# A two-layer hybrid attention step on one core: bias table in contiguous runs; scaling, shifting and evacuation moved to ScalarE, low parts to VectorE

## The reference

```python
def rms_norm(x, g):
    y = xf * lax.rsqrt(jnp.mean(xf * xf, axis=-1, keepdims=True) + EPS)
    return y * g
def modulate(x, g, shift, scale):
    return rms_norm(x, g) * (1 + scale[:, None, :]) + shift[:, None, :]
def gated_residual(x, y, g, gate):
    return x + gate[:, None, :] * rms_norm(y, g)
def channel_mixer(h, w1, w2):
    return jnp.square(jax.nn.relu(h @ w1)) @ w2
...
# per layer, for the context tokens (c_ctx) and the latent tokens (c):
h = modulate(x, g[0], shift0, scale0)
y = mixer(h)      # layer 0: retention heads || neighbourhood attention; layer 1: latent attention
x = gated_residual(x, y, g[1], gate)
h = modulate(x, g[2], shift1, scale1)
x = gated_residual(x, channel_mixer(h, w_mlp_in, w_mlp_out), g[3], gate1)
# neighbourhood attention adds to each score a value of a table of 15 x 31 per head:
bias = rpb[:, dr, dc]; bias = jnp.where(valid, bias, NEG_INF)
```

## Time and profile before

| | us |
|---|---|
| three runs | 2003.93, 2004.2, 2000.57 (median 2003.93) |
| the profiled execution | 2003.88 |
| its span | 2002.1 |
| TensorE busy | 1825.5 (91%) |
| VectorE busy | 1160.4 (58%) |
| ScalarE busy | 698.1 (35%) |
| GpSimd busy | 272.1 (14%) |

### The profile page before, as it was taken

How to read it: one execution, slowest core, us unless ns; L and a number is a source line. 1 busy time by engine, 2 the same in 40 slices (tenths; PEclk the granted TensorE clock), 3 DMA queues, 4 the chain that set the end, 5 groups by cost and what they waited for, 6 DMA issues and landing times.

```text
span 2002.1 us, 28780 instructions
## 1 busy us (share of the span) xinstructions
PE 1825.5 (91%) x11572; PEld 1647.5 (82%) x11572; DVE 1160.4 (58%) x2017; ACT 698.1 (35%) x1179; POOL 272.1 (14%) x262
## 2 busy tenths in 40 slices
PE   7899988379879999999988899999898999999998
PEld 3799853259779999999977886777787999999997
DVE  2777557364776676767574765565457653233345
ACT  2332234154442222313333454555444313132233
POOL 2200000142420000000242120011242000000012
PEclk9799989589889999999988799999998899999999
DMA  8244320102334545444331020000132442222232
GB/s 293 88 158 148 105 62 12 43 1 87 93 98 134 159 136 155 140 153 142 106 88 56 27 85 1 1 1 1 56 103 74 131 122 74 75 73 82 72 111 74
DMA packets 274605, 181.32 MB, mean 91 GB/s; under 512 B 23029, under 2 KB 249130, under 8 KB 274474
## 3 DMA queue, kind: packets, MB, share of 16 engines
q1 hardware_dynamic: 274474, 179.50, 29.3%
HBM read 175.92 MB, written 3.56 MB: 90 GB/s over the span
## 4 chain that ended last, share of the span: by engine, by line
PE 70%; DVE 11%; issue 5%; SPq 5%; ACT 5%; POOL 3%; DMA 1%; ACTq 0%; POOLq 0%; DVEq 0%
PE ps L630 18%; PE ps L632 18%; PE ps L631 18%; SPq L552 4%; PE ps L1099 4%; PE ps L1077 3%; DVE nt L1570 2%; ACT w_hi L414 2%; PE ps L1088 2%; PE ps L701 1%; DVE w_lo L423 1%; DVE nt L1568 1%; POOL rstd L2101 1%; DVE xT L1558 1%; PE ps L762 1%
## 5 line engine op out<-in xcount | busy, mean ns | idle before, releaser
L630 PE MATMUL ps<-hM_hi,w_lo 128*128 128x320 f32 x1120 | 361.9, 323 | 36.2 <-POOL hM_lo L2105 20.7
L414 ACT ACTIVATE w_hi<-stage 128x1024 fp32r<-128x1024 f32 (+2 forms) x230 | 239.2, 1040 | 405.3 <-PE ps L632 355.8
L423 DVE TENSOR_TENSOR w_lo<-stage,w_hi 128x1024 fp32r<-128x1024 f32 (+2 forms) x230 | 281.5, 1224 | 164.8 <-ACT w_hi L414 162.9
L630 PE MATMUL ps<-h_hi,w_lo 128*128 128x320 f32 x1152 | 359.8, 312 | 4.7 <-DVE w_lo L423 4.6
L632 PE MATMUL ps<-h_hi,w_hi 128*128 128x320 f32 x1152 | 357.2, 310 | 0.0
L631 PE MATMUL ps<-h_lo,w_hi 128*128 128x320 f32 x1152 | 357.1, 310 | 0.0
L631 PE MATMUL ps<-hM_lo,w_hi 128*128 128x320 f32 x1120 | 355.0, 317 | 0.0
L632 PE MATMUL ps<-hM_hi,w_hi 128*128 128x320 f32 x1120 | 354.6, 317 | 0.0
L630 PEld LDWEIGHTS ps<-hM_hi,w_lo 128*128 128x128 f32 x1120 | 216.7, 194 | 49.5 <-POOL hM_lo L2105 27.7
L2101 POOL TENSOR_TENSOR rstd<-rstd,sq 128x320 f32<-128x320 f32 x98 | 118.3, 1207 | 990.6 <-ACT sq L1148 987.5
L630 PEld LDWEIGHTS ps<-h_hi,w_lo 128*128 128x128 f32 x1152 | 217.0, 188 | 9.5 <-DVE w_lo L423 7.4
(11 more groups left out here) (287 smaller groups left out, 2928.3 us busy)
## 6 DMA issues: line engine op xcount, KB each, us to landing
stage<-in_w_mlp_in SPq DMA_DIRECT2D x76, 512.0 KB, 4.0
stage<-in_w_mlp_out SPq DMA_DIRECT2D x76, 512.0 KB, 4.2
slab_mlp<-in_w_ada SPq DMA_DIRECT2D x28, 1024.0 KB, 5.1
stage<-in_w_in_ac SPq DMA_DIRECT2D x28, 512.0 KB, 3.7
slab_ac<-in_w_ada SPq DMA_DIRECT2D x12, 1024.0 KB, 5.9
ada_a<-in_w_ada SPq DMA_DIRECT2D x8, 1024.0 KB, 8.6
stage<-in_w_out_ac SPq DMA_DIRECT2D x14, 512.0 KB, 4.1
stage<-in_w_out_c SPq DMA_DIRECT2D x14, 512.0 KB, 4.0
```

Source lines behind the costliest of these rows:

```text
L414: nc.scalar.activation(w_hi[:, n % 2, 0:width], stage[:, n % STAGE, 0:width], ACT.Copy)\
L423: nc.vector.tensor_tensor(w_lo[:, n % 2, 0:width], stage[:, n % STAGE, 0:width], w_hi[:, n % 2, 0:width].bitcast(F32), ALU.subtract).then_ ...
L630: mm(out, lo[:, k], xh, start=j == 0, stop=False)
```

## The change

1. The bias table has rows of 8 x 31 words without gaps, 272 words per head. Each of the 128 DMAs puts 8 runs of 248 words instead of 64 runs of 31. GpSimd reads the window with a hand-built view that steps 31 words from key row to key row.
2. A modulated tile: VectorE makes the product with the spread factor; ScalarE scales and shifts it twice, into the high part and, in place, into `nt`; VectorE subtracts for the low part. GpSimd has no part in it.
3. `project_out`: ScalarE squares PSUM directly and then copies it into `yT`; VectorE has no part in it.
4. At units 0, 5, 6 and 7 of the first up stage of each layer, GpSimd and not VectorE makes the plain square `s2`.

```diff
-STAGES = (..., ("out0", 8, "sweeps", "d"),
+STAGES = (..., ("out0", 8, "sweeps", "a"),      # who evacuates; out1 likewise
+BIAS_W = ROWS * RPB_C + 24
+POOL_SQUARES = (0, 5, 6, 7)
-        [bias] = lay(80, ("bias", [P, NH, ROWS, 48], F32))
+        [bias] = lay(80, ("bias", [P, NH, BIAS_W], F32))
-                    sp.dma_start(bias[q:q + 1, :, :, c + 1:c + 1 + RPB_C],
-                                 rpb[0:1, :, ROWS - 1 - r:2 * ROWS - 1 - r, :]).then_inc(na_bias_in, 16)
+                    sp.dma_start(bias[q:q + 1, :, c + 1:c + 1 + ROWS * RPB_C],
+                                 rpb[0:1, :, ROWS - 1 - r:2 * ROWS - 1 - r, :].rearrange("l h r c -> l h (r c)"))
+                        .then_inc(na_bias_in, 16)
 # ScalarE
-                f(out[:, k, half(s)], nt[:, k % 2, half(s)], ACT.Copy).then_inc(h_hi_done[s], 1)
+                for dst, done in ((out, None), (nt, h_hi_done[s])):
+                    for a, b, g in HALVES[s]:
+                        to = dst[:, k, a:b] if done is None else dst[:, k % 2, a:b]
+                        last = f(to, nt[:, k % 2, a:b], ACT.Identity, scale=coef[:, layer, which, k, g:g + 1],
+                                 bias=mod[:, layer, 8 * shift + k, g:g + 1])
+                last.then_inc(h_hi_done[s], 1)
 # ScalarE, project_out, every unit u
-                    if u:
-                        y_square(y_name, name, u - 1)
+                    act.wait_ge(unit_done, g + 1)
+                    square(y_name, s, u % 8, single(g))
+                    f(yT[:, j, half(s)], single(g), ACT.Copy).then_inc(act_evac, 1)
 # VectorE
-                link(tt(nt[:, k % 2, cols], xT[:, k, cols], spread(name, s), ALU.mult))
-                for a, b, g in HALVES[s]:
-                    last = ts(nt[:, k % 2, a:b], nt[:, k % 2, a:b], coef[...], mod[...], ALU.mult, ALU.add)
-                last.then_inc(h_full[s], 1)
+                tt(nt[:, k % 2, cols], xT[:, k, cols], spread(name, s), ALU.mult).then_inc(h_full[s], 1)
+            def low_part(name, s, k, hi, lo):
+                dve.wait_ge(h_hi_done[s], KD * MOD_NO[name] + k + 1)
+                tt(lo[:, k, cols], nt[:, k % 2, cols], hi[:, k, cols].bitcast(F32), ALU.subtract)
+                    .then_inc(h_lo_done[s], 1)
+            def modulate(name, s, k, hi, lo):
+                normalise(name, s, k)
+                if k:
+                    low_part(name, s, k - 1, hi, lo)
+                if k == KD - 1:
+                    low_part(name, s, k, hi, lo)
 # GpSimd
-                        bias[:, 2 * m + e, :, u:u + KW].rearrange("p r c -> p c r"),
+                        bias_window(2 * m + e, u),
+                at = bias[:, h, u:u + 1]
+                return bass.AP(at.tensor, at.offset, [at.ap[0], [1, KW], [RPB_C, ROWS]])
```

More of the change, by code:

```diff
@@ L1156, in square_root, with operand @@
                     .then_inc(root_done[s], 1)
-            def operand(name, s, k, out):
+            def operand(name, layer, which, shift, s, k, out):
                 act.wait_ge(h_full[s], KD * MOD_NO[name] + k + 1)
-                f(out[:, k, half(s)], nt[:, k % 2, half(s)], ACT.Copy).then_inc(h_hi_done[s], 1)
+                for dst, done in ((out, None), (nt, h_hi_done[s])):
[4 more added lines that the diff above has]
+                last.then_inc(h_hi_done[s], 1)
             def y_square(name, stage, u):
@@ L1200, in _ @@
             for k in range(KD):
-                square("in0", 0, k, xT[:, k, :])
+                square("in0", 0, k, xT[:, k, half(0)])
             mod_rows(5)
             for k in range(KD):
-                square("in0", 1, k, xT[:, k, :])
+                square("in0", 1, k, xT[:, k, half(1)])
             mod_rows(6)
@@ L1211, in _ @@
                 for s in range(2):
-                    operand("in0", s, k, hA_hi)
+                    operand("in0", 0, A1, SHIFT1, s, k, hA_hi)
             def row_copy(p, bank):
@@ L1439, in _ @@
                     act.wait_ge(act_evac, EVAC[g][0])
-                    square("cq", s, (u - 3) % 3, cT[:, j, :])
+                    square("cq", s, (u - 3) % 3, cT[:, j, half(s)])
                 elif u >= 10:
@@ L1560, in residual, with normalise @@
                 last.then_inc(x_done[s], 1)
-            def modulate(name, layer, which, shift, s, k):
+            def normalise(name, s, k):
                 cols = half(s)
@@ L1675, in _ @@
             dve_split(dve, 0)
-            for k in range(KD):
+            for k in range(KD + 1):
                 for s in range(2):
-                    modulate("in0", 0, A1, SHIFT1, s, k)
+                    if k < KD:
+                        normalise("in0", s, k)
+                for s in range(2):
+                    if k:
+                        low_part("in0", s, k - 1, hA_hi, hA_lo)
             y, w, ln, z, z2, s, big, out = [lg[:, n, :] for n in range(8)]
@@ L1916, in mlp @@
                             for k in (6, 7):
-                                modulate(*x, u // 8, k)
+                                modulate(x, u // 8, k, hM_hi, hM_lo)
+                        if c == 0 and u == 0:
+                            dve.wait_ge(act_evac, EVAC[UNIT_AT[f"out{layer}"] + 15][0])
                         split_next(name, u)
@@ L1927, in mlp @@
                         dve.wait_ge(act_evac, EVAC[g][0])
-                        link(tt(s2[:, v % 2, cols], r32[:, v % 2, cols], r32[:, v % 2, cols], ALU.mult))
+                        if c == 0 and u in POOL_SQUARES:
+                            dve.wait_ge(s2_done, len(POOL_SQUARES) * layer + POOL_SQUARES.index(u) + 1)
+                        else:
+                            link(tt(s2[:, v % 2, cols], r32[:, v % 2, cols], r32[:, v % 2, cols], ALU.mult))
                         v += 1
@@ L2110, in _ @@
                     add_square("in0", s, k)
-            for k in range(KD):
-                for s in range(2):
-                    low_part("in0", s, k, hA_hi, hA_lo)
             pool.wait_ge(v_done, 8)
```

112 lines of the change are left out of this document (53 added, 59 removed), and 2 rows, old and new, of the table STAGES.

## The result

The changed kernel takes 2012.92 us (median of 4 runs, 2012.1 to 2014.41); beside it the kernel before took 2002.25 us (4 runs). The ratio is 1.0055, 95% interval 1.0038 to 1.0073: 11 us slower. The forecast was 1993.4 us, 1970 to 2005 the range; the time lies outside it, and on the other side of the kernel before. It is rival B's side, in a milder form.

What follows compares the result with a forecast made beforehand. TensorE's work and still stretches bound the kernel, longest its wait behind SP's bias DMAs. From 2003.88 us, -29.7 (bias) + 2.8 + 1.9 + 2 x 2.45 + 2 x 4.8 (norms) = -10.5 gave 1993.4 us, range 1970 to 2005.

Steps and rivals of the forecast that it cites:

- rival B: SP's bias DMAs: issue time stays, a price of the instruction, so the norms' 19.2 us stand alone: 2023 us; chance 0.12.
- What bounded the kernel: TensorE's work plus its still stretches; longest wait 30.4 us, behind SP's 128 bias issues and the mask.
- the price of an issue: SP's bias loads: 0.432 us an issue instead of 0.666, ending at 345.5 us, taking 29.7 us off.
- The break-even of 0.52 us: SP's bias issue time at which the saved wait just pays the norms' 19.2 us; upward, the change is slower.
- The norms: Scaling tiles and evacuating on ScalarE, in in0, in_c, the up stages, out0 and out1: a cost of 19.2 us.
- in0: First unit of the input projection: a tile pair takes 2.96 us against 2.52, +2.8 us in all.
- in_c: Half 1, first high part to last low part: 15.2 us against 13.3, +1.9; half 0 costs 0.
- up00 and up10, units 6 to 8: Modulated tiles on ScalarE: +0.95 us from unit 6's split to its evacuation, +1.5 to the last low part, +2.45 a layer.
- the evacuation: out0 and out1, square and copy on ScalarE: 0.75 us a unit, free at units 0 to 7, +4.8 a layer.
- the scaling as a whole: Modulated tiles on ScalarE in in0, in_c, up00 and up10, without the evacuation: forecast 9.6 us.
- The signs to look for: Right: bias issues near 0.43 us, out0 splits 5.7 apart; wrong: issue above 0.55, splits still 4.9 apart.
- Rival A: Norm stretches: scaling and evacuation on ScalarE cost nothing, TensorE-bound stretches swallow the rest; 1974 us; chance 0.2.

Runs made afterwards that it cites:

- experiment 6: Kernel before, norms as before, with the bias table built ahead in DRAM by a fill and 8 loads, then loaded once: 1973.48 us, ratio 0.9855.
- experiment 7: Kernel before, norms as before, with the new bias table and its 128 loads issued half by SP, half by GpSimd: 1974.06 us, ratio 0.9853.
- experiment 1: Kernel before with the new bias table and its 8-run loads alone, norms as before: 1997.89 us, ratio 0.9975.
- experiment 2: Changed kernel with the old bias table and its old loads, so the new norms and evacuations alone: 2016.13 us, ratio 1.0070.
- experiment 10: Changed kernel, its norms and evacuations kept, with the bias table built in DRAM and loaded at once: 1985.48 us, ratio 0.9922.
- experiment 9: Kernel before with the new bias table and the evacuation of out0 and out1 on ScalarE; scaling, shifting, low parts as before: 2009.45 us, ratio 1.0044.
- experiment 8: Changed kernel with the evacuation of out0 and out1 back on VectorE, squares one unit later: 2002.89 us, ratio to the kernel before 1.0011.
- experiments 3 and 4: Kernel before with the new bias table filled by loads of several forms, other values; only issue times read, 0.243 us for one run into one partition.
- experiment 5: Kernel before, norms as before, with 128 bias loads of one 14 KB run each into a flat table: 1979.32 us, ratio 0.9888.

## Why the prediction was wrong

**What bounded the kernel** was read rightly. That the whole of L912's wait is SP's issuing, and that VectorE is late next, at 355.5, is shown by experiments 6 and 7: 29 us of the forecast's 29.7 are there to be had, by two ways that share nothing but the end of the issues.

**The failed step is the price of an issue**, "I take 0.432, as the new form has little in it but its start". It was 0.620, and the term was -5 us (experiment 1) instead of -29.7. Both ends of the range were named (0.273 and 0.666), and the value between them was taken from rows whose form was another: c_ctx and kpos spread over 8 and 128 partitions, one run in each. The nearest row by form was the old bias load itself, also cut runs inside one partition, and the state loads beside it had already said that the count of runs does not set the price. That was cited, and given 12%. For an issue the cutting of a row mattered and the size did not: 8 x 8 runs of 62 KB cost 0.306 and one run of 7.9 KB 0.243. The rule of the Trainium skill that was cited beside it, "DMA: Bandwidth & Descriptors", section "Rules for kernel authors" (under 64 KB mostly overhead, coalesce), named the better remedy; the runs agree, as the one load of 1.1 MB of experiment 6, with its eight loads ahead, took 29 us away.

**Rival B** had the place and the direction. Its mechanism, "a price of the DMA instruction and not of its runs", is half right: an issue can cost 0.243 us, so 0.38 of the 0.62 is not the instruction's but comes with cutting one row into runs. Its 2023 was high, as the issue did fall by 7% and the norms were cheaper. The break-even of 0.52 us, reckoned with norms of 19.2, was right in kind: 0.62 is above it and the kernel is slower.

**The norms**, that is scaling and evacuation together, forecast +19.2, cost 14 alone (experiment 2), 13 beside the DRAM table (experiment 10), 16 beside the new loads (after less experiment 1, by the ratios). By steps, from the ledger:
- in0, +2.8: measured +2.4 in the changed kernel (from 0.2 to 2.6), 2.5 and 2.6 in two others with it, 0 to 0.4 in three without. Right.
- in_c, +1.9: the last low part starts at 1074.01, so it ends 1.2 us later than before, of which 0.6 was there at the start: +0.6. The tile in half 1 takes ScalarE 1.65 us (1059.87 to 1061.53 and so on), not 1.80: its four instructions are some 0.03 shorter than supposed. And 1.61 to 1.82 from one high part to the next had been the pace before. Between 1010 and 1050 us, ahead of in_c, five of the six columns give 0.8 to 1.8 us back, "bias table alone" among them: it is the clock and not the edit (in the unit at 1010 us it is 0.77 in the kernel before and 1.00 in these five).
- up00 and up10, units 6 to 8, +2.45 each: from the split of unit 6 to its evacuation 7.70 us for 7.25 (+0.45, forecast 0.95), and in up00 the last low part ends 13.3 behind that for 12.8 (+0.5, forecast 1.5). The ledger has +0.9 from the split of unit 6 to that of unit 8 in both layers. The reason is the same. The further 1.2 of the table behind up00 (589 us) stand in "table by DRAM" too, and half of them in "bias table alone".
- the evacuation, +4.8 a layer: 3.0 in out0, 6.7 in out1, 9.7 for 9.6 in sum (experiment 9). Units 9 to 12 gave 2.6 each time and unit 8 nothing (forecast for 8 to 12 3.9: the period went to 5.63, not 5.7, and in two of the four units only to 5.33 and 5.36); units 14 and 15 gave 0.5 and 0.2 (forecast 0.8 and 0.6). The rest was made up by the first unit (0.6, which the forecast held for covered) and by unit 13 of out1, +2.7, at TensorE's lower clock, which the forecast had only in its upper bound. The sum is right by luck: its parts are not.
- the scaling as a whole, without the evacuation: forecast 9.6. Experiment 8 less experiment 1 gives +7 us, the changed kernel less experiment 9 +2, and the steps above 4.9; its size is known no better than that.

**The signs to look for** served: the issue above 0.55 us was named as what would make it wrong. Rival A (norms free) is out, by all columns. With the right issue price the forecast would have been 2003.9 - 5.7 + 19.2 = 2017: that one number is 24 us, more than the whole miss of 19.5, and the norms, priced too dear by 3 to 6 us, hid part of it.

## What to carry over

Price a DMA issue by the nearest row of the same form (how many partitions, and one run or several in each), not by the row nearest in bytes or count; a cut row and a whole row differ more than 8 runs and 64. Where a queue is the wait, first ask who else could issue: moving half of the loads to an idle engine took one loop and gave all of it, and the new shape of the loads gave a sixth. And put nothing on the engine that is late already: some 0.7 us a unit of evacuation on ScalarE came back as 9 to 14 us.

## What the runs showed of the hardware

- Issue time on SP's queue: 0.243 us for one run into one partition (1 KB or 7.9 KB), 0.559 for two runs, 0.620 for eight, 0.657 for sixty-four; 0.264 for 2 partitions x 8 runs, 0.306 for 8 x 8; 0.597 for 64 partitions x 64 bytes (experiments 3 and 4).
- GpSimd issues the 8-run load in 0.518 us, for 0.620 on SP (experiment 7).
- 128 loads of one run of 14 KB into one partition (experiment 5): they start 0.29 us apart up to 310 us, then 0.52 to 0.53, and the next issue took 15.7 us, at 28 GB/s and 7% busy engines.
- ScalarE's instruction with scale and bias from tensors takes 0.648 us for 320 columns (changed kernel), against 0.471 for the one with none (kernel before). The function differs too, Identity for Copy; the two were not separated.
- TensorE at its lower clock from 1487 to 1497 us of the changed kernel, 36 matmuls in 8 us for 60. Unit 13 of out1 takes 6.62 us, at a granted clock of 0.50, in four kernels alike.
